# A dense feed-forward with seven products per pair of weight tiles: three of the four weight sums made by accumulating DMA, and every low part made by VectorE

## The reference

```python
def swiglu(h, w_gate, w_up, w_down):
    return (jax.nn.silu(h @ w_gate) * (h @ w_up)) @ w_down
...
    h = rmsnorm(x, norm_ffn[layer])
    if layer % 2 == 0:
        x = x + swiglu(h, ffn_w_gate[j], ffn_w_up[j], ffn_w_down[j])   # D_MODEL 1024, D_FF 2816
```

## Time and profile before

| | |
|---|---|
| runs, median (lowest to highest) | 1552.4 us (1552.14 to 1553.08) |
| span of the profiled execution, on its own clock | 1550.1 us |
| TensorE busy | 1529.5 us (99%) |
| VectorE busy | 1099.5 us (71%) |
| ScalarE busy | 872.2 us (56%) |
| GpSimd busy | 333.7 us (22%) |
| share of TensorE in the chain that ended last | 93% |
| mean granted TensorE clock | 0.998 |

### The profile page before, as it was taken

One profiled execution on the slowest core, in us unless ns is written; L12 is line 12 of the kernel. 1 busy time (PEld: TensorE's weight loads), 2 busy tenths in 40 slices (PEclk: granted clock), 3 DMA queues, 4 the chain that ended last, 5 costly groups with the idle time before them and its releaser, 6 DMA issues.

```text
span 1550.1 us, 24600 instructions
## 1 busy us (share of the span) xinstructions
PE 1529.5 (99%) x8392; PEld 1321.4 (85%) x8393; DVE 1099.5 (71%) x1784; ACT 872.2 (56%) x1418; POOL 333.7 (22%) x350
## 2 busy tenths in 40 slices
PE   8999999999999999999999999999999999999997
PEld 6888888888999988887888888879898888889895
DVE  7657765758989963436657766776676998887587
ACT  5436665335445442224347764565576888886564
POOL 0204564003544600002015662010000011110000
PEclk9999999999999999999999999999999999999999
DMA  6732212242453233336322112519777999997773
GB/s 221 205 99 69 64 66 82 83 149 84 161 182 131 89 123 91 98 105 153 108 78 80 59 63 88 190 65 327 254 254 256 364 383 373 391 376 267 239 257 132
DMA packets 89793, 265.79 MB, mean 171 GB/s; under 512 B 12497, under 2 KB 22737, under 8 KB 89680
## 3 DMA queue, kind: packets, MB, share of 16 engines
q1 hardware_dynamic: 82864, 248.59, 47.0%
q0 software_dynamic: 6816, 15.74, 3.5%
HBM read 242.84 MB, written 19.83 MB: 169 GB/s over the span
## 4 chain that ended last, share of the span: by engine, by line
PE 93%; DVE 3%; ACT 1%; DMA 1%; issue 1%; SPq 0%; DVEq 0%; ACTq 0%; POOLq 0%
PE ps L1978 14%; PE ps L1983 14%; PE ps L1979 14%; PE ps L2384 8%; PE ps L2359 5%; PE ps L2361 5%; PE ps L2360 5%; PE ps L2386 3%; PE ps L2264 2%; PE ps L2265 2%; PE ps L2272 2%; PE ps L2145 2%; PE ps L2233 2%; PE ps L2234 2%; PE ps L2238 2%; PE ps L2178 1%
## 5 line engine op out<-in xcount | busy, mean ns | idle before, releaser
L973 ACT ACTIVATE w_hi<-raw 128x1024 fp32r<-128x1024 f32 (+1 forms) x124 | 129.3, 1043 | 214.2 <-PE ps L1983 211.1
L1978 PE MATMUL ps<-h_hi,w_hi 128*128 128x512 f32 x544 | 219.9, 404 | 1.0 <-DVE h_lo L1395 0.6
L1979 PE MATMUL ps<-h_lo,w_hi 128*128 128x512 f32 x544 | 212.9, 391 | 0.0
L1983 PE MATMUL ps<-h_hi,w_lo 128*128 128x512 f32 x544 | 212.7, 391 | 0.0
L1375 DVE TENSOR_TENSOR m_lo<-m_raw,m_hi 128x1024 fp32r<-128x1024 f32 x144 | 167.9, 1191 | 58.8 <-ACT m_hi L1016 50.9
L1370 DVE TENSOR_TENSOR w_lo<-raw,w_hi 128x1024 fp32r<-128x1024 f32 (+1 forms) x94 | 112.9, 1201 | 101.6 <-ACT w_hi L973 96.7
L1016 ACT ACTIVATE m_hi<-m_raw 128x1024 fp32r<-128x1024 f32 x144 | 145.3, 1031 | 54.2 <-PE ps L2358 25.9
L2384 PE MATMUL ps<-xt,m_hi 128*128 128x320 f32 x592 | 154.3, 347 | 0.3 <-issue 0.3
L2386 PE MATMUL ps<-xt,m_lo 128*128 128x160 f32 x592 | 140.3, 237 | 0.0
L1983 PEld LDWEIGHTS ps<-h_hi,w_lo 128*128 128x128 f32 x544 | 102.1, 188 | 22.4
L1375 DVE TENSOR_TENSOR m_lo<-h_rows,m_hi 128x1024 fp32r<-128x1024 f32 (+1 forms) x96 | 102.0, 1087 | 22.1 <-ACT m_hi L1016 21.7
(11 more groups left out here) (371 smaller groups left out, 4066.9 us busy)
## 6 DMA issues: line engine op xcount, KB each, us to landing
m_raw<-moe_g SPq DMA_DIRECT2D x88, 512.0 KB, 5.4
raw<-w_in SPq DMA_DIRECT2D x68, 512.0 KB, 3.3
m_raw<-moe_down SPq DMA_DIRECT2D x56, 512.0 KB, 5.7
raw<-w_gu SPq DMA_DIRECT2D x44, 512.0 KB, 3.9
h_rows<-moe_g SPq DMA_DIRECT2D x32, 512.0 KB, 5.1
h_rows<-moe_g SPq DMA_DIRECT2D x32, 384.0 KB, 4.7
h_rows<-moe_down SPq DMA_DIRECT2D x24, 512.0 KB, 5.6
m_raw<-moe_g SPq DMA_DIRECT2D x24, 384.0 KB, 5.4
```

What stands on the lines that cost most here:

```text
L973: A.activation(split_of(n, 0, cols)[0], raw[:, n % RAW, 0:cols], ACT.Copy).then_inc(hi_ready, 1)
L1978: E.matmul(ps[:, bank, :], wh, hi, start=first, stop=False)
L1979: E.matmul(ps[:, bank, :], wh, lo, start=False, stop=False)
L1983: return E.matmul(ps[:, bank, :], wl, hi, start=False, stop=final)
```

## The change

GpSimd keeps one sum of a seven. The up row of the block matrix is taken with turned sign, so that all four weight sums become additions: s1 = up low + up high, s2 = s1 + gate low, s3 = gate low + up low, s4 = s2 + gate high. s1, s3 and s4 are made by DMAs that GpSimd issues and that add what they read from `w_gu` in DRAM onto a tile: s1 onto the raw up low, s3 onto the raw gate low (after job 0 has used it), s4 onto s2's tile (after job 1 has used it). The turned sign is taken back in the token sums and in the gate product (`scalar=-1.0`). VectorE makes all seven low parts. Jobs 2 and 3 change places (and banks), so two names of PSUM banks change (`SEVEN_AT`, `pair_banks`). Semaphores of the first loads of x and of the last loads of y are merged (`block_in`), which changes names in later places and no order.

```diff
-            return ((gate, low), (None, 1), (None, 2), (None, 0), (gate, high), (up, high), (None, 2))[j]
+            return ((gate, low), (None, 0), (up, low), (gate, low), (gate, high), (up, high), (None, 0))[j]
...
-        SEVEN_AT = (0, 2, 6, 4, 1, 3, 7)
+        SEVEN_AT = (0, 2, 4, 6, 1, 3, 7)
...
-            return {0: (0, 1), 1: (4, 5), KF - 1: (4, 5)}.get(f, (0, 2))
+            return {0: (0, 1), 1: (4, 5), KF - 1: (4, 5)}.get(f, (0, 3))
...
-                        sp.wait_ge(seven_lo_pool, SEVENS.index(f) + 1)
...
-            def weight_sums(q, part):
...
-            def low_on_pool(q):
...
+            def first_sums(q):
...
+                pool.wait_ge(raw_full[(n + 1) % RAW], 16 * ((n + 1) // RAW + 1))
+                pool.dma_start(up[:, 0:T], w_gu[2 * f + 1][:, T:UNIT], accum_op=ALU.add).then_inc(s1_added, 16)
+                pool.wait_ge(raw_full[n % RAW], 16 * (n // RAW + 1))
+                if q >= len(sums):
+                    pool.wait_ge(seven_lo, LOW_COUNT[JOB[("seven", SEVENS[q - len(sums)], 6)]])
+                pool.wait_ge(s1_added, 16 * (q + 1))
+                pool.tensor_tensor(sums[q % len(sums)][:], up[:, 0:T], gate[:, 0:T], ALU.add).then_inc(sums_ready, 1)
+
+            def later_sums(q):
...
+                pool.wait_ge(sums_ready, q + 1)
+                pool.wait_ge(seven_lo, LOW_COUNT[JOB[("seven", f, 0)]])
+                pool.dma_start(raw[:, (FFN_START + 2 * f) % RAW, 0:T], w_gu[2 * f + 1][:, 0:T], accum_op=ALU.add).then_inc(s3_added, 16)
+                pool.wait_ge(seven_lo, LOW_COUNT[JOB[("seven", f, 1)]])
+                pool.dma_start(sums[q % len(sums)][:], w_gu[2 * f][:, T:UNIT], accum_op=ALU.add).then_inc(s4_added, 16)
...
-                    for part in range(3):
-                        weight_sums(0, part)
...
+                    for q in range(len(SEVENS)):
+                        first_sums(q)
+                        later_sums(q)
...
+                        if kind == "seven" and j == 1:
+                            A.wait_ge(sums_ready, SEVENS.index(f) + 1)
+                        if kind == "seven" and j in (2, 3, 6):
+                            A.wait_ge({2: s1_added, 3: s3_added, 6: s4_added}[j], 16 * (SEVENS.index(f) + 1))
                         A.activation(job_split(x)[0], job_full(x), ACT.Copy).then_inc(seven_hi, 1)
...
+                        if f in SEVENS:
+                            V.scalar_tensor_tensor(out=act_of(f), in0=up, scalar=-1.0, in1=silu_of(f),
+                                                   op0=ALU.mult, op1=ALU.mult).then_inc(act_ready, 1)
...
                         for y in FREED_BY[x]:
-                            if not on_pool(y):
-                                job_low(y)
+                            job_low(y)
...
-                            E.wait_ge(t_lo_ready, (2, 4, 6, 0, 8)[j - 1])
+                            E.wait_ge(t_lo_ready, (2, 6, 6, 0, 8)[j - 1])
...
-                        if on_pool(x):
-                            E.wait_ge(seven_lo_pool, q + 1)
-                        else:
-                            E.wait_ge(seven_lo, LOW_COUNT[x])
+                        E.wait_ge(seven_lo, LOW_COUNT[x])
```

## The result

The changed kernel takes 1579.5 us (median of 4 runs, 1576.0 to 1579.9) beside 1552.3 us of the kernel before (1550.4 to 1553.1). The ratio is 1.0174 [1.0158, 1.0189]: slower by 27 us, and 19.5 us above the top of my range of 1549.0 to 1560.0. The forecast was wrong.

A forecast was written before the change was run, and what follows sets the result against it. TensorE was taken to bound the steady rounds. Steady rounds 0, first round -2.0, the rest unchanged: span 1550.1 to 1548.1 us, plus 2.3 carried from the runs' median, 1550.4 us, "no change"; range 1549.0 to 1560.0.

The forecast's parts named there:

- D: Time from issue to landing of a 256 KB accumulating DMA, put between 2.4 and 5.7 us and taken as 4.0.
- My upper bound of 5.7: Longest landing of the sync queue's 512 KB weight loads, taken as the most a 256 KB accumulate would need.
- (A): Rival, chance 0.28: accumulates outlast their cover at product 3 of even sevens; 1556.4 us at D = 5.0, 1564 at 5.7.
- The odd cover: Product (7,3) of the odd seven: no wait for s3 up to D = 5.9, or about 5 beside loads.
- The even seven: Product (6,3), thinnest cover: can start at 404.6 + 2D, 1.0 us ahead of need; cover ends at D = 4.5.
- First round: Around the first seven: 3.05 us of waits go, one of 1.1 comes at product 3, so 2.0 us gained.
- VectorE's relief: In steady rounds VectorE's busy share comes down from 92% to some 75%, with subtractions at 0.68 us.
- (C): Rival, chance 0.04: VectorE is not freed, held by DMA issues and the kept sum; 30.8 of 31.0 us a round, 1555.
- The estimate of 3.2 us: Landing of a 256 KB accumulate by the fit, 2.0 us plus twice 256 KB at 436 GB/s; no steady-round waits.
- The ceiling: TensorE's lost time, all in the first round: 3.05 us, 0.20% of the time, is the most to gain.

The follow-up runs named there:

- The best of the changed kernels: The changed kernel with s3 made by GpSimd in its own tile and the 16 zero fills moved to the down-weight loads: 1551.8 us, 1.0004.

## Why the prediction was wrong

**The step that failed** is "I take D = 4.0", used for every accumulate, and with it the cover given to the odd seven, "Cover to D = 5.9, or about 5 where the loads of f = 8 share the engines".

- **D.** 4.0 is right for an accumulate in a quiet place: s3 of the even seven took 4.0 to 4.4. Under SyncE's loads and fills s3 of f = 4, 7, 10, 13 took 7.79, 6.45, 6.43 and 8.05, s1 up to 7.8. My upper bound of 5.7 came from SyncE's 512 KB loads, which in that trace had no GpSimd traffic beside them; it was no upper bound for a DMA issued right after 1.5 MB of others. That a fill goes out with each pair of loads stands in the kernel, and I left it out. The argument against (A) looked at 407 to 415 us, where the DMA engines are 1% busy; that is the even seven's place. The same trace shows the odd seven's: SyncE sends two loads and a fill from 416.5 to 417.9, where I had s3 issued at about 417.1, and the DMA engines are 62% busy from 416 to 424:

```profile
416.53 0.81 SPq L566 DMA_DIRECT2D raw<-w_gu  x2
417.38 0.52 SPq L618 DMA_DIRECT2D y_dram<-bias_t  x1
416.00:424.00 8.00, 8.00 (x69) 8.00 (x69) 7.72 (x9) 3.62 (x7) 5.68 (x4) 1.00 0.62 198
```

- **The odd cover.** Waits of 3.67, 2.32, 2.32 and 3.94 at those four D give a cover of 4.1 each time, not 5.9 or 5. At f = 7 I had the low part of (7,0) 2.1 us after the end of (6,3). It came 3.9 us after (about 420.2 to 424.14): ahead of it in VectorE's queue stand the activation's low part (1.81 beside the kept sum, itself late after s1), another low part and an addition. Then s3's issue starts 0.55 us after that low part, a hand-over that I had at nothing. Together that is 2.3 less cover; 0.7 of it came back, as TensorE's own short waits made (7,3) due later.
- **The even seven.** Its path was right, place and formula: s1 + kept sum + s3, 9.0 us for both transfers. At f = 9 they took 7.3 (441.39 to 448.7) and 4.1, 2.4 over; the gap was 2.61. Rival (A) named this place and the chain, but priced both at one D below 5.7 (1564). What it lacked was the way back: a late low part delays the reload, and this the next s1.
- **The odd seven was no rival at all**, and it had the larger sum, 12.3 us against 8.9.
- **The clock** I left out. It cost 5.8 us more, all of it behind waits. The 0.26 us that each gap costs beyond its bracket I had not counted either.
- **First round.** Right up to product 3: the wait at 376.00 went (first seven at 374.89), s3 was issued at 374.07, landed by 378.3 (predicted 378.5), and the gap at product 3 is 0.95 (predicted 1.1). Then the odd seven f = 4 took more than all of it.
- **VectorE's relief.** 61% of the steady stretch in the changed kernel, but of a longer time; in the kernel without waits (s3 by GpSimd, fills moved) 117.95 of 154.6 us, 76%, for my 75%. Against (C), the subtractions beside DMA issues took 0.68 (that of 425.26 beside the issue of 425.27), and the one beside the kept sum 1.81. The Trainium skill's rule on two-input VectorE instructions ("SBUF — State Buffer", section "Who interferes with whom") thus holds here in both halves.
- **The cost of adding.** A plain load of 256 KB took 2.9 us at least, the added one 4.0. The estimate of 3.2 us from the fit in the Trainium skill ("DMA: Bandwidth & Descriptors", section "Anatomy of one DMA") is too low even alone. What the Trainium skill says of adding ("Collectives: The Full Stack", section "The bandwidth ceiling: the fold count and why AG ≠ RS ≠ AR") agrees in its direction, and the size here is 1.1 us; that the second read is the reason no run shows.
- **The ceiling.** "3.05 us is the most this change can bring" stands: no variant beat the kernel before by more than its measurement can tell. The best of the changed kernels, 1551.8, takes none of the 3.05: it has 2.0 us of waits in the first round, where the kernel before has 1.7.

Open: where within the DMA path (GpSimd's queue or the 16 engines) an accumulate waits behind SyncE's bytes; no run separates the two. Open too is how the loss of the kernel with s1 and s3 by GpSimd divides.

## What to carry to other kernels

Give each occurrence of a DMA on the path its own duration, by what the other queues have sent just before it; a transfer that nothing waits for, as a zero fill, counts there. Where the need comes 4 us after the issue, as for s3 here, an engine's 1.3 us addition is a safer producer than an accumulating DMA of 4 to 8 us; but not for every sum, as GpSimd's additions slow the VectorE low parts beside them (four sums by GpSimd: 1558 to 1559 us). Work out a cover with every instruction that stands ahead in the releasing engine's queue, and follow a delay once around the loop (low part, reload, next sum) before pricing it.

## What the hardware showed that I had not expected

An accumulating DMA of 256 KB from DRAM onto SBUF lands in 4.0 us at best, a plain one in 2.9; GpSimd's issue of it takes 0.87 us against 0.55. With 1.5 MB sent just ahead by another queue it took 6.4 to 8.05 us, with 1 MB 4.6 to 5.7, and with those transfers held back until it had landed 4.6 at most.

TensorE's granted clock fell to 0.50 around a gap of 3.67 us. It fell to 0.50 too behind the gap of 3.94, after 1.2 us of work at 1.00, and behind one of 2.07 (at 533.09), but not behind those of 2.32, 2.61 and 2.76 us. With SyncE's loads held it fell behind gaps of 2.78, 2.56 and 2.68 us and not behind one of 2.70. So the length of the last gap alone does not decide it.
